# First attention of a two-block layer: run inside its projection instead of behind it, with an output projection by token tiles

## The reference

```python
h = rms_norm(x, norm1_g); proj = h @ w_in              # 1024 -> 3072
q_d, k_d, v_d, q_m, k_m, v_m = split(proj)             # six groups of 512 columns
# differential attention, 4 heads with 2 maps each, head width 64, values 128 wide
q, k = rms_norm(q_d, q_g), rms_norm(k_d, k_g)          # per head
p = softmax(where(dist >= 0, q k^T / 8 + bias[bucket(dist)], -1e30))
out_d = rms_norm((p[:, 0] - lam * p[:, 1]) @ v_d, sub_g) * (1 - lambda_init)
# block attention, 8 heads; with 256 tokens it is causal attention with a bias
out_m = softmax(masked q_m k_m^T / 8 + bias) @ v_m     # q_m, k_m normed per head
x = x + concat(out_d, out_m) @ w_out                   # then norm2, router, 32 experts (top 2 of a group)
```

## Time and profile before

| what | value |
|---|---|
| median of 3 runs | 1102.63 us (1102.37 to 1106.66) |
| the profiled execution | 1103.3 us, span of its instructions 1101.6 us |
| PE busy | 1040.7 us, 94% of the span |
| DVE / ACT / POOL busy | 556.0 / 428.2 / 51.5 us |
| mean granted TensorE clock | 0.979 |
| DMA | 239.60 MB, 218 GB/s mean |

### The profile page before, as it was taken

The page is one execution under the profiler, slowest core; times in us unless marked ns, Lnnn a source line. Parts: engine busy times, 40 slices in busy tenths (PEclk is TensorE's granted clock), DMA queues, the critical chain, the costliest instruction groups (busy, mean ns, idle before and its releaser), DMA issues.

```text
span 1101.6 us, 13370 instructions
## 1 busy us (share of the span) xinstructions
PE 1040.7 (94%) x5377; PEld 799.0 (73%) x5377; DVE 556.0 (50%) x844; ACT 428.2 (39%) x564; POOL 51.5 (5%) x57
## 2 busy tenths in 40 slices
PE   7997999999999999999999999978999999999997
PEld 6885886654444448778788899856788888877875
DVE  5577454222222255444445647587755655444443
ACT  4456232322222143443444444384344344444342
POOL 2430000000000000000000000010100000000000
PEclk9999899999999999999999999888999999999999
DMA  8872375999999957555555555311175636555540
GB/s 287 265 260 112 153 308 207 369 421 418 422 421 421 421 199 253 191 159 184 190 171 173 175 189 189 124 70 39 41 246 191 191 115 221 180 190 156 187 152 39
DMA packets 101821, 239.60 MB, mean 218 GB/s; under 512 B 11666, under 2 KB 56810, under 8 KB 86282
## 3 DMA queue, kind: packets, MB, share of 16 engines
q1 hardware_dynamic: 99850, 229.05, 57.3%
q0 software_dynamic: 1920, 9.85, 2.6%
HBM read 237.81 MB, written 3.43 MB: 219 GB/s over the span
## 4 chain that ended last, share of the span: by engine, by line
PE 79%; DVE 7%; ACT 6%; issue 5%; POOL 1%; DVEq 0%; ACTq 0%; POOLq 0%
PE banks L1038 18%; PE banks L1040 17%; PE banks L1039 17%; PE banks L1268 8%; PE banks L1293 5%; ACT weights_hi L666 4%; PE banks L1248 3%; PE banks L1277 3%; DVE stage L2025 1%; PE banks L1045 1%; PE banks L1183 1%; PE banks L1392 1%; PE banks L1055 1%; PE banks L1152 1%; ACT stage L744 1%
## 5 line engine op out<-in xcount | busy, mean ns | idle before, releaser
L1687 DVE TENSOR_TENSOR weights_lo<-raw_weights,weights_hi 128x2048 fp32r<-128x2048 f32 x116 | 265.8, 2292 | 216.8 <-ACT weights_hi L666 216.6
L666 ACT ACTIVATE weights_hi<-raw_weights 128x2048 fp32r<-128x2048 f32 x116 | 221.8, 1913 | 175.4 <-PE banks L1040 160.0
L1038 PE MATMUL banks<-weights_hi,normed_T_hi 128*128 128x512 f32 (+1 forms) x624 | 247.6, 397 | 9.8 <-DVE stage L2025 7.5
L1040 PE MATMUL banks<-weights_hi,normed_T_lo 128*128 128x512 f32 (+1 forms) x624 | 243.0, 389 | 0.0
L1039 PE MATMUL banks<-weights_lo,normed_T_hi 128*128 128x512 f32 (+1 forms) x624 | 242.1, 388 | 0.0
L1038 PEld LDWEIGHTS banks<-weights_hi,normed_T_hi 128*128 128x128 f32 x624 | 118.1, 189 | 40.8 <-DVE stage L2025 13.3
L1040 PEld LDWEIGHTS banks<-weights_hi,normed_T_lo 128*128 128x128 f32 x624 | 117.7, 189 | 25.0
L1039 PEld LDWEIGHTS banks<-weights_lo,normed_T_hi 128*128 128x128 f32 x624 | 117.9, 189 | 22.6
L1038 PE MATMUL banks<-weights_hi,ffn_hidden_T_hi 128*128 128x512 f32 x160 | 62.4, 390 | 0.0
L1040 PE MATMUL banks<-weights_hi,ffn_hidden_T_lo 128*128 128x512 f32 x160 | 62.3, 389 | 0.0
L1039 PE MATMUL banks<-weights_lo,ffn_hidden_T_hi 128*128 128x512 f32 x160 | 62.2, 389 | 0.0
(11 more groups left out here) (356 smaller groups left out, 1673.0 us busy)
## 6 DMA issues: line engine op xcount, KB each, us to landing
raw_weights<-in_w_in SPq DMA_DIRECT2D x38, 1024.0 KB, 5.0
raw_weights<-in_ffn_w_gate SPq DMA_DIRECT2D x44, 512.0 KB, 3.9
raw_weights<-in_ffn_w_up SPq DMA_DIRECT2D x44, 512.0 KB, 4.9
raw_weights<-in_ffn_w_down SPq DMA_DIRECT2D x22, 1024.0 KB, 4.7
stage<-in_w_down SPq DMA_DIRECT2D x14, 1024.0 KB, 11.8
expert_weights<-in_w_gate SPq DMA_DIRECT2D x12, 1024.0 KB, 11.0
expert_weights<-in_w_up SPq DMA_DIRECT2D x12, 1024.0 KB, 13.6
expert_weights<-in_w_down SPq DMA_DIRECT2D x12, 1024.0 KB, 14.5
```

The costliest lines, as they stand in the source:

```text
L666: ins = eng.activation(w_hi[:, slot, :], raw, ACT.Copy)
L1038: eng.matmul(dst, x[0], w[0], start=first_one, stop=False)
L1040: return eng.matmul(dst, x[1], w[0], start=False, stop=last_one)
L1687: ins = eng.tensor_tensor(w_lo[:, slot, :], raw, w_hi[:, slot, :], ALU.subtract)
```

## The change

The column groups are computed in the order q_d, k_d, q_m, k_m, v_d, v_m (position p = 0..5 takes the place of c). Scores are issued in six bursts between quarters (a piece for one tile) of groups p = 3, 4, 5; DVE's logits and ACT's exponentials stand between their weight splits. `hs` rows 3 and 4 hold the head sums of the projection, since rows 0 to 2 are in use by the softmax at the same time. Transposed weights and values products stay behind the projection, in finer steps, without the 20 idle matmuls. The output projection is issued by quarters, tile 0 first. On POOL the spreading of the bias table goes ahead of the first roots, and the skewed read ahead of the second.

```diff
+W_ORDER = (0, 1, 3, 4, 2, 5)
+        BURSTS = [(0, range(0, 4), 6), (1, range(0, 2), 6), (1, range(2, 4), 6),
+                  (0, range(4, 8), 6), (1, range(4, 6), 4), (1, range(6, 8), 6)]
...
             eng.dma_start(bias_row, bias_stage).then_inc(bias_stored, 16)
-            head_roots()
             eng.wait_ge(bias_stored, 16)
             eng.dma_start(bias_rows, bias_row.rearrange("h m -> (h m)").partition_broadcast(P)).then_inc(bias_stored, 16)
             head_roots()
...
             eng.dma_start(bias, skewed).then_inc(bias_loaded, 16)
+            head_roots()
...
+            qk_squares(2)
+            feed(6)
+            for t in range(TILES):
+                qk_copy(1, t)
+            feed(7)
+            first_exps(1, 0, 0)
+            qk_squares(3)
+            feed(8)
+            for t in range(TILES):
+                qk_copy(2, t)
+            feed(9)
+            qk_copy(3, 0)
+            first_exps(2, 1, 0)
+            qk_copy(3, 1)
+            feed(10, BEFORE_MOE)
+            first_exps(3, 0, 1)
+            first_exps(4, 1, 1)
+            pT_copy((0, 0))
+            pT_copy((0, 1))
+            feed(11, BEFORE_MOE)
+            heads_squared(0)
+            feed(12, BEFORE_MOE)
+            t8_split(T_Y, yT, vec[:, V_SUB:V_SUB + 1], (0,))
+            heads_squared(1)
+            t8_split(T_Y, yT, vec[:, V_SUB:V_SUB + 1], (1,))
             feed(13, BEFORE_MOE)
...
+            def first_scores(b):
+                t, gs, _ = BURSTS[b]
+                n = P * (t + 1)
+                eng.wait_ge(qk_done, (2 if b < 3 else 6) + t + 1)
+                if b in (1, 2, 3):
+                    eng.wait_ge(score_used, BURST_START[b])
+                elif b == 5:
+                    eng.wait_ge(score_used, BURST_START[4])
...
+                        if p in (1, 2, 3) and kh == 1 and t == 1:
+                            for tile in range(TILES):
+                                qk_transpose(p - 1, tile)
+                        if (p, kh, t) == (3, 0, 1):
+                            first_scores(0)
+                        if (p, kh, t) == (3, 1, 1):
+                            first_scores(1)
+                        if (p, kh, t) == (4, 0, 1):
+                            first_scores(2)
+                            qk_transpose(3, 0)
+                        if (p, kh, t) == (4, 1, 0):
+                            qk_transpose(3, 1)
+                        if (p, kh, t) == (4, 1, 1):
+                            first_scores(3)
+                        if (p, kh, t) == (5, 0, 0):
+                            first_scores(4)
+                        if (p, kh, t) == (5, 0, 1):
+                            first_scores(5)
...
-                if t == 0:
-                    stay_warm(20, 7)
...
+            eng.wait_ge(score_used, 8 * TILES)
+            first_weights(0)
+            weights_copied((0, 0))
+            eng.wait_ge(proj_used, 5 * TILES)
+            first_values(0, range(4))
+            eng.wait_ge(proj_used, 6 * TILES)
+            first_values(0, range(4, 12))
+            first_weights(1)
+            weights_copied((0, 1))
+            first_values(1, range(8))
+            transpose8_tile(0, tok, (mixed, 2), False)
+            first_values(1, range(8, 12))
...
+            eng.wait_ge(t8_lo, TILES * T_Y + 1)
+            w_out_part(0, 0, 0)
+            w_out_part(0, 1, 0)
+            transpose8_tile(1, tok, (mixed, 4), False)
+            w_out_part(1, 0, 0)
+            eng.wait_ge(t8_lo, TILES * T_Y + 2)
+            w_out_part(0, 0, 1)
+            w_out_part(0, 1, 1)
+            w_out_part(1, 0, 1)
+            w_out_part(1, 1, 0)
+            w_out_part(1, 1, 1)
...
+            head_squares_of(2)
+            feed(6)
+            take_projection(2)
+            eng.wait_ge(bias_loaded, 16)
+            first_logits(0)
+            feed(7)
+            first_logits(1)
+            head_squares_of(3)
+            feed(8)
+            take_projection(3)
+            first_logits(2)
+            feed(9)
...
             differential_weights(0)
+            first_logits(3)
+            take_projection(4)
+            first_logits(4)
+            feed(10, BEFORE_MOE)
+            first_logits(5)
+            differential_weights(1)
             pT_copy((0, 0))
-            differential_weights(1)
+            take_projection(5)
             pT_copy((0, 1))
+            feed(11, BEFORE_MOE)
             normed_heads(0)
+            feed(12, BEFORE_MOE)
+            t8_split(T_Y, yT, vec[:, V_SUB:V_SUB + 1], (0,))
             normed_heads(1)
-            t8_split(T_Y, yT, vec[:, V_SUB:V_SUB + 1])
+            t8_split(T_Y, yT, vec[:, V_SUB:V_SUB + 1], (1,))
             feed(13, BEFORE_MOE)
```

More of the change, by code:

```diff
@@ L385, in z_piece, with burst_place @@
             return first["w_in_2"] + 2 * Z_ORDER.index(g)
+        BURSTS = [(0, range(0, 4), 6), (1, range(0, 2), 6), (1, range(2, 4), 6),
+                  (0, range(4, 8), 6), (1, range(4, 6), 4), (1, range(6, 8), 6)]
+        BURST_START = [sum(len(gs) for _, gs, _ in BURSTS[:b]) for b in range(len(BURSTS) + 1)]
+        EXP_START = {(0, 0): 0, (1, 0): 8, (0, 1): 16, (1, 1): 24}
+        def burst_place(b, x):
+            t, _, bank = BURSTS[b]
+            n = P * (t + 1)
+            return bank, slice(x * n, (x + 1) * n)
         def score_bank(t, g):
@@ L703, in _ @@
             feed(0)
[L706 to L722, removed]
+            def qk_copy(p, t):
+                n = TILES * p + t
+                if n == 0:
+                    eng.wait_ge(vec_ready, 1)
+                eng.wait_ge(qk_ps, n + 1)
+                eng.activation(qkT[p][:, :, t * P:(t + 1) * P], PS[:, 4 + n % 2, :].rearrange("p (j q) -> p j q", j=4),
+                               ACT.Copy, scale=vec[:, V_QK + p:V_QK + p + 1]).then_inc(qk_done, 1)
@@ L1114, in _, with qk_transpose @@
-            for c in range(6):
-                if c == 1:
+            def qk_transpose(p, t):
+                n = TILES * p + t
+                eng.wait_ge(proj_used, n + 1)
+                if n >= 2:
+                    eng.wait_ge(qk_done, n - 1)
+                for b in range(4):
+                    mm = eng.transpose(PS[:, 4 + n % 2, b * P:(b + 1) * P], tok[:, t, b * P:(b + 1) * P], ident[:, :])
+                mm.then_inc(qk_ps, 1)
+            def first_scores(b):
+                t, gs, _ = BURSTS[b]
+                n = P * (t + 1)
+                eng.wait_ge(qk_done, (2 if b < 3 else 6) + t + 1)
[3 more added lines that the diff above has]
+                    eng.wait_ge(score_used, BURST_START[4])
+                for x, g in enumerate(gs):
+                    q, k = qkT[2 * (g // 4)][:, g % 4, :], qkT[2 * (g // 4) + 1][:, g % 4, :]
+                    bank, at = burst_place(b, x)
+                    for m in range(2):
+                        rows = slice(HEAD * m, HEAD * (m + 1))
+                        mm = eng.matmul(PS[:, bank + m, at], q[rows, t * P:(t + 1) * P], k[rows, 0:n], start=True, stop=True)
+                    mm.then_inc(score, 1)
@@ L1806, in masked_logits @@
                 n = P * (t + 1)
-                for g in range(8):
-                    eng.wait_ge(score, 8 * t + g + 1)
-                    b = score_bank(t, g)
+                eng.wait_ge(score, BURST_START[b + 1])
+                for x, g in enumerate(gs):
+                    bank, at = burst_place(b, x)
                     for m in range(2):
                         head = g if g < 4 else DIFF_HEADS + 2 * (g - 4) + m
-                        ins = add_and_max(t, 2 * g + m, b + m, bias[:, head, SEQ - n:], LEAST)
+                        ins = add_and_max(t, 2 * g + m, PS[:, bank + m, at], bias[:, head, SEQ - n:], LEAST)
```

180 lines of the change are left out of this document (88 added, 92 removed).

## The result

The changed kernel took 1098.92 us (median of 16 runs, 1095.0 to 1104.14), the kernel before 1105.09 us (16 runs, 1099.62 to 1108.17). The ratio is 0.9949, 95% interval [0.9934, 0.9964]: it is faster, by 0.5%. Forecast were 1093 us, that is 0.9% off the 1102.63 us known then; the measured time is 5.9 us over the forecast and just inside the stated range of 1090 to 1099. The 16 runs of the kernel before lie in two groups, eight from 1099.62 to 1103.88 and eight from 1106.29 to 1108.17 us, and both the 1102.63 and the profile that the prediction started from are of the lower one.

A forecast was written before the change was run, and what follows sets the result against it. Taken as bound: a chain through the attention, 41.44 us between the projections with no engine full. From 1103.3 us, 11.8 gained and 2.1 for the clock gave 1093.6, stated as 1093 us; range 1090 to 1099.

The forecast's parts named there:

- The projection's end: PE ends the projection at 95.7: 87.1 plus 7.5 for scores, 0.9 for transposes, 0.2 for restarts, no waiting.
- the step on the bias table: POOL starts the spreading at about 31 instead of 37; the table lands near 55 and costs nothing.
- (b): ACT's 8 exponentials precede the last k group's squares; tile 0's scaling ends at 74.6, when PE gets there: slack nought.
- (c): In the projection's end, the last logits end at 91.8 and the second combination at 95.1, PE at 95.7.
- (a): PE's second score burst needs the first logits, behind scaling, squares and piece 7; the chain arrives about 1 us before PE.
- The rival "projection waits": DVE is at 88% of the projection stretch and a tight place misses: 3 to 7 us more, 1096 to 1100; chance 0.22.
- the rival "piece 7 late": Bias spreading beside pieces 6 and 7 makes piece 7 land after 52, PE waiting; 1106 us, chance 0.03.
- The gap ahead of the transposes: PE idles 3.7 us, 108.5 to 112.2, while DVE splits piece 13 before norming tile 0's heads.
- The clock: PE's clock falls once at the tail's gap, for 3.4 to 6.9 us, costing 2.1 us (bounds 0 and 3.5).
- The output projection: It takes 22.8 us: 21.9 plus 0.9 for tile 1's transposes between its quarters, other waits covered.
- rival of 0.06: The expert stage's DMA stream is the bound from a fixed time on and takes the gain: 1103 us; chance 0.06.
- signs named beforehand: Among the signs of being right: SP's wait on the experts' gate matmuls, 26.4 us before, is shorter or equal.

The follow-up runs named there:

- experiment 1: Changed kernel with POOL's old order put back (first head roots before the spreading of the bias, second ahead of the skewed read): 1095.92 us.
- experiment 3: Changed kernel with SP's three small loads (w_if, b_if, sink) moved ahead of weight piece 3, early spreading kept: 1098.95 us.
- experiment 6: Changed kernel with 28 idle matmuls on PE in the gap ahead of tile 0's transposes: 1099.63 us.
- experiment 5: Changed kernel with tile 0's head norm ahead of piece 13's split, and piece 14's split behind that of the transposed rows: 1093.66 us.
- experiment 10: Changed kernel with POOL's old order and tile 0's head norm ahead of piece 13's split: 1091.8 us.
- experiment 2: Kernel before with only POOL's new order (spreading of the bias first, second head roots behind the skewed read): 1103.84 us.
- experiment 4: Changed kernel with SP's three small loads ahead of piece 3 and piece 6 ahead of the router's loads: 1097.23 us.
- experiment 9: Changed kernel with the output projection's quarters undone, tile 1's values whole and both tiles transposed together before it: 1100.83 us.

## Why the prediction was off

**The projection's end (forecast 95.7, 0 us of waiting).** The sum was right: 95.40 in experiment 1, with POOL's old order and all else of the change, and 96.0, 95.6 and 96.1 in the three others with that order. What failed is the step on the bias table, put at nothing: that the spreading, started at 31 "in a stretch where the DMA engines have room", "costs nothing", and that "on SP nothing changes but the columns". The table's own landing was forecast well (near 55; 42.16 + 14.1 = 56.3). Its neighbours weren't looked at: SP's small loads, which stood at 31 to 33 in the program before, now coincide with it, and the queue behind them stood; and where the issues were short (experiment 3) the pieces shared the DMA engines with it and were late as well. Nor was the room there that the step counted on. The kernel before moved few bytes in that stretch, but its DMA engines were already busy for 0.77 and 0.52 of the time (the first two windows). In the changed kernel they were idle for a third of the time while `b_if`'s issue kept the pieces back (the third):

```profile
31.00:34.00 3.00, 3.00 (x15) 2.49 (x14) 2.32 (x5) 2.10 (x2) 2.10 (x2) 1.00 0.77 53
34.00:37.00 3.00, 3.00 (x15) 2.49 (x14) 2.06 (x3) 1.29 (x1) 2.92 (x1) 1.00 0.52 124
37.00:42.00 5.00, 5.00 (x28) 4.22 (x27) 3.22 (x3) 1.53 (x3) 0.00 (x0) 1.00 0.68 161
```

The profiles of the changed order gave 100.2, 101.6, 97.6 and 98.5 for a program that is the same up to there, so its price was 2 to 6 us and changed between executions; the old order kept within 0.7.

**The tight places.** (b) and (c) cost nothing, as taken (in the profiles of experiments 3 and 6 PE waited 0.62 and 0.45 us at (b)). (a) was the right kind of place, one step off: I had looked at the second burst behind the squares behind piece 7 and found 1 us in hand. The first burst hangs on `qk_copy(1)`, which ACT has behind its split of piece 8, and that is where the lateness came out. The rival "projection waits" gave 1096 to 1100, which is where the time lies, but by DVE's load, so that it met the number with a mechanism that did not occur; the rival "piece 7 late" had the mechanism, a piece landing after 52, but at 0.03 and only for the extreme case. The two belonged together, with far more weight.

**The gap ahead of the transposes.** Forecast 3.7 us by DVE's order, measured 3.68; ends at 16.23 us behind the projection's end, forecast 16.5. Right, and experiment 5 shows that the order was its cause.

**The clock.** It fell in the tail as forecast, but for longer: it stood at its lower level from 114 to 124, where the prediction had 3.4 to 6.9 us. Mis-sized with that was the price: 2.6 by experiment 6 instead of 2.1. The output projection without it takes 23.2 instead of 22.8. The prediction had weighed what the Trainium skill says in "TensorE: Matmul & The Clock Gate", section "HAM oscillation — how this bites in real kernels", that such gaps bring the lower clock back each time. The trace agrees for the tail's gap of 3.68 us. In the projection, where no gap was forecast, the clock fell behind 2.76 us too and cost 1.7; but it did not fall behind every gap of the projection (last section).

**Behind it.** From the end of the output projection to the first gate matmul 27.15 us passed, 25.72 before. In both the clock was at its lower level for as long (1.7 us of work lost between 150 and 180), but before that lay on idle matmuls ahead of the wait for DVE's `assign`, now on the gathering's matmuls. The prediction had nothing for it. The same instructions take 25.7 us in five of the twelve profiles, 26.3 in four and 27.2 in the three (changed kernel, experiments 6 and 10) in which the lower clock lay on the gathering. From there on 925.2 us, before 925.3: the expert stage took nothing, as forecast (rival of 0.06). Between its first row (0.81) and 173.0 ACT's timeline has no table load. One of the signs named beforehand missed by a little: SP's longest wait for the gate matmuls was 27.3 us, not 26.4 or less.

Together: +4.5 for the projection, +0.6 for tail and output, +1.4 for the routing, -0.1 behind it, 6.4 us over the forecast span of 1091.9: 1098.3, measured 1098.2.

## What to carry to other kernels

- When a transfer is moved in time, list what every other queue issues in its new place, not only when the moved one lands: here one transfer, moved 7 us ahead, cost 3 to 4 of the 9.6 us that the change was reckoned to bring (projection's end at 99.5 as the mean of four profiles, 95.8 with the old order; medians 1098.92 and 1095.92), and its old place had been harmless.
- When scores or other small work moves into a full stream of matmuls, its operands' copies inherit every wait of the engine that makes them. Follow that engine's program back to the last transfer it waits for.
- On the engine that feeds the end of a stage, put what the next matmul waits for ahead of splits that are wanted later: that order alone was worth 4.9 us up to the first output matmul, more than the quarters (1.2).

## What was not expected of the hardware

- An issue on SP's queue can be long for a small load: 8 KB took 8.50 us to issue (8.59 in experiment 2) beside the spreading of 2304 KB by POOL's queue, and 0.66 without it; four router loads 12.89 instead of 6.98 us. The loads that stretched are written in small pieces (`b_if` is one short row repeated on 128 partitions); weight pieces of 1024 KB were issued in 0.4 to 2.0 us beside the same spreading. That the small pieces are the reason was not tried.
- The clock didn't fall after every gap in the projection: after 2.76, 2.77 and 3.17 us it did (changed kernel, experiments 4 and 5), after 1.08, 1.17 and 2.23 us it did not (experiments 6, 3 and 9).
- The same instructions behind the first attention take 924.8 to 927.7 us from kernel to kernel, in step with the clock lost around the second attention (13.6 to 17.0 us). A gain of 2 or 3 us ahead can be hidden or enlarged by it.
